# First 2 MB of up weights behind the thirtieth pass: one transfer of 48 rows and ten of 8 rows

## The reference

```python
def moe_ffn(x, w_router, b_router, w_up, b_up, w_down, b_down):
    logits = (x @ w_router + b_router).astype(jnp.float32)
    top_v, top_i = lax.top_k(logits, TOP_K)
    gates = jax.nn.softmax(top_v, axis=-1)
...
    for e in range(N_EXPERTS):
        hid = x @ w_up[e] + b_up[e]
        x_glu = jnp.minimum(hid[..., ::2], SWIGLU_LIMIT)
        x_lin = jnp.clip(hid[..., 1::2], -SWIGLU_LIMIT, SWIGLU_LIMIT)
        act = x_glu * jax.nn.sigmoid(SWIGLU_ALPHA * x_glu) * (x_lin + 1.0)
        out = out + gate_full[:, e:e + 1] * (act @ w_down[e] + b_down[e])
    return out
```

## Time and profile before

| | us |
|---|---|
| median of 3 runs (lowest, highest) | 1095.09 (1094.93, 1096.48) |
| the profiled execution, device time | 1095.05 |
| the profiled execution, span | 1093.3 |
| TensorE matmul busy (share of the span) | 1041.1 (95%) |
| VectorE, ScalarE busy | 254.1, 194.4 |
| SyncE's queue of transfers: bytes, share of 16 engines' span | 427.17 MB, 93.4% |

### The profile page before, as it was taken

One profiled execution on the slowest core, in us unless ns is written; L12 is line 12 of the kernel. 1 busy time (PEld: TensorE's weight loads), 2 busy tenths in 40 slices (PEclk: granted clock), 3 DMA queues, 4 the chain that ended last, 5 costly groups with the idle time before them and its releaser, 6 DMA issues.

```text
span 1093.3 us, 12731 instructions
## 1 busy us (share of the span) xinstructions
PE 1041.1 (95%) x5191; PEld 457.5 (42%) x5191; DVE 254.1 (23%) x660; ACT 194.4 (18%) x365; POOL 8.0 (1%) x25
## 2 busy tenths in 40 slices
PE   8999999999999999999999998999999999999995
PEld 8988564333333333333333333333333333333331
DVE  6887354111111111111111111011111111111113
ACT  5584221111111111111011111011111110111110
POOL 2000000000000000000000000000000000000000
PEclk9999999999999999999999999999999999999998
DMA  9725798999999999999999999999999999999993
GB/s 324 222 77 152 291 403 332 383 430 428 430 427 434 433 429 433 429 432 430 432 430 432 430 432 430 432 430 431 432 427 436 424 437 427 435 430 424 427 423 150
DMA packets 36000, 428.33 MB, mean 392 GB/s; under 512 B 3888, under 2 KB 17232, under 8 KB 20112
## 3 DMA queue, kind: packets, MB, share of 16 engines
q1 hardware_dynamic: 34416, 427.17, 93.4%
q10 hardware_dynamic: 1536, 0.43, 0.2%
HBM read 426.02 MB, written 1.05 MB: 391 GB/s over the span
## 4 chain that ended last, share of the span: by engine, by line
PE 64%; DMA 34%; DVE 1%; ACT 0%; issue 0%; ACTq 0%; DVEq 0%; SPq 0%
DMA ring<-in_w_down_dram 23%; PE bank L1506 22%; PE bank L1570 15%; DMA wbuf<-in_w_down_dram 7%; PE bank L1461 4%; PE bank L1208 4%; PE bank L1446 3%; PE bank L1225 3%; DMA tail_mem<-in_w_down_dram 3%; PE bank L1271 3%; PE bank L1454 1%; PE bank L1550 1%; PE bank L1517 1%; PE bank L1536 1%; PE bank L1189 1%; PE bank L1253 1%
## 5 line engine op out<-in xcount | busy, mean ns | idle before, releaser
L1506 PE MATMUL bank<-ring,wbuf 128*64 128x512 f32 x1248 | 276.9, 594 | 1.9 <-DMA ring<-in_w_up_dram 1.2
L1570 PE MATMUL bank<-ring,wbuf 128*64 128x512 f32 x640 | 146.5, 610 | 18.0 <-DMA ring<-in_w_down_dram 18.0
L1506 PEld LDWEIGHTS bank<-ring,wbuf 128*64 128x64 f32 x1248 | 87.7, 137 | 164.8 <-issue 156.4
L698 ACT ACTIVATE wbuf<-wbuf 128x256 f32<-128x256 f32 x64 | 26.6, 416 | 474.0 <-DVE wbuf L1133 474.0
L1133 DVE TENSOR_SCALAR wbuf<-bank 128x256 f32<-128x256 f32 x64 | 26.8, 420 | 309.3 <-PE bank L1506 309.3
L1117 DVE TENSOR_SCALAR hT<-iota_s,hT 128x128 f32<-128x128 f32 x64 | 19.3, 344 | 334.5 <-PE bank L1536 333.4
L1570 PEld LDWEIGHTS bank<-ring,wbuf 128*64 128x64 f32 x640 | 50.0, 141 | 111.6 <-issue 109.4
L1506 PE MATMUL bank<-tail_mem,wbuf 128*64 128x512 f32 x416 | 93.1, 594 | 0.9 <-DMA tail_mem<-in_w_up_dram 0.9
L1506 PE MATMUL bank<-wbuf 128*64 128x512 f32 x384 | 85.8, 594 | 0.0
L1461 PE MATMUL bank<-wbuf,putT 64*128 64x512 f32 x264 | 65.6, 615 | 1.4 <-ACT wbuf L703 1.4
L1446 PE MATMUL bank<-X,hT 128*64 128x512 f32 x256 | 60.9, 593 | 0.1
(11 more groups left out here) (244 smaller groups left out, 814.6 us busy)
## 6 DMA issues: line engine op xcount, KB each, us to landing
ring<-in_w_up_dram SPq DMA_DIRECT2D x29, 4096.0 KB, 40.8
ring<-in_w_down_dram SPq DMA_DIRECT2D x14, 4096.0 KB, 37.4
ring<-in_w_up_dram SPq DMA_DIRECT2D x20, 2048.0 KB, 16.0
wbuf<-in_w_up_dram SPq DMA_DIRECT2D x10, 4096.0 KB, 40.7
tail_mem<-in_w_up_dram SPq DMA_DIRECT2D x9, 4096.0 KB, 39.6
ring<-in_w_down_dram SPq DMA_DIRECT2D x10, 2048.0 KB, 17.7
wbuf<-in_w_down_dram SPq DMA_DIRECT2D x5, 4096.0 KB, 38.1
tail_mem<-in_w_up_dram SPq DMA_DIRECT2D x8, 2048.0 KB, 19.3
```

The costliest lines, as they stand in the source:

```text
L698: a.activation(sig[:, w], glu[:, w], ACT.Sigmoid, scale=SIG_ALPHA).then_inc(s["sig_ready"], 1)
L1506: ins = mm(bank[n][c * SLOTS:(c + 1) * SLOTS, :], xT[:, k, :], units(row, n, c), start=(k == 0), stop=(k == KT - 1))
L1570: ins = mm(bank[1 if last else 2][c * SLOTS:(c + 1) * SLOTS, :], actT[:, at:at + SLOTS], wk[:, a * D + c * 512:a * D + (c + 1) * 512], sta ...
```

## The change

In the loop, the first of the four up chunks is no longer one transfer of 128 rows but eleven: rows 0 to 47, then ten times 8 rows. All go to the same buffer and raise the same semaphore, each by 16, so TensorE's wait for this chunk asks for 176 a pass where it asked for 16, and the raise before the loop is adapted. The other three up chunks, the down chunks and all passes before are as they were.

```diff
+        ROW_PARTS = [slice(0, 48)] + [slice(r, r + 8) for r in range(48, P, 8)]
...
                 for c in range(UPC):
                     sp.wait_ge(s["chunk_used"], p * CHUNKS + used(up_at(1, c)) - CHUNKS)
-                    sp.dma_start(buffer(UP_HOME[c]), source(e, c)).then_inc(chunk_in[UP_HOME[c]], 16)
+                    for r in ROW_PARTS if c == 0 else [slice(0, P)]:
+                        sp.dma_start(buffer(UP_HOME[c])[r, :], source(e, c)[r, :]).then_inc(chunk_in[UP_HOME[c]], 16)
...
-                pe.wait_ge(chunk_in[UP_HOME[c]], 16 * p + 16)
+                each = 16 * (len(ROW_PARTS) if c == 0 else 1)
+                pe.wait_ge(chunk_in[UP_HOME[c]], each * p + each)
                 return buffer(UP_HOME[c])
...
-            for b in UP_HOME:
-                pe.sem_inc(chunk_in[b], 16 * (FIXED + 1 - seen[b]))
+            for c, b in enumerate(UP_HOME):
+                pe.sem_inc(chunk_in[b], 16 * (len(ROW_PARTS) if c == 0 else 1) * (FIXED + 1) - 16 * seen[b])
```

## The result

The change made the kernel slower: 1111.53 us (median of 4 runs, 1109.02 to 1113.26) against 1095.01 for the kernel before in the same session. The ratio is 1.0156, with a 95% interval of 1.0143 to 1.0169. The forecast was 1092.8 and the range ended at 1098.5. Of these, 1.2 us had been lost before the change begins (its first issue stands at 1023.99, where the one of before stands at 1022.77, a difference between executions); 17.0 us belong to the change.

What follows compares the result with a forecast made beforehand. The prediction took the weight stream's landing at 1062.28, set by the later half of the DMA engines, to bound the end. 5.5 - 3.05 - 0.15 = 2.3 us earlier gave 1095.09 - 2.3 = 1092.8 us; range 1092.3 to 1098.5.

Steps and rivals of the forecast that it cites:

- the price of a row: Weight stream: each 16,384-byte row is one packet done by one engine, 0.611 us a row.
- Where the rows go: Changed chunk: eight engines get 13 rows, the others 3; one half falls back 3.05 us, the other gains 3.05.
- the sum's only term for what the ten transfers cost the engines: Overhead of ten more transfers on the eight engines getting the rows: 0.15 us, bounds 0 and 0.8.
- the eight of an 8-row transfer being all ahead: Main case, chance 0.74: 8-row transfers use the engine half that ends first, so landings come earlier.
- the other half or a mix: Rival, chance 0.20: 8-row transfers include late engines; later landings 3.2 us later, total 1098.3.
- the term of 2.45 us: Landing that stood at 1062.28: 5.5 - 3.05 = 2.45 us earlier, before overhead.
- a shelf of some 11 us at one half: Wrong-half sign at the stream's end: DMA share stays at 0.5 for some 11 us.
- the prediction's instruction fetches: Supposed source of the lag: 31 fetches of 16 KB between 200 and 1070, seemingly all carried by eight engines.
- In a row: Rival, chance 0.01: each 8-row transfer begins when the one before has landed, 2.1 us each; total 1108.
- 0.5 us an issue: SyncE's issues of the split chunk: 0.52 us each, 5.2 us for ten more, hidden by the queue.
- is there well before 1045.11: TensorE's wait on the split first chunk: the chunk lands before TensorE needs it, so no wait.
- The 5.5 us lag: Weight stream: eight of sixteen DMA engines run 5.5 us behind the other eight, and they set each landing.

Runs made afterwards that it cites:

- extra_own: Kernel before plus five additional 8-row transfers into a free buffer, rows four apart within rows 0 to 63; 1097.19 us.
- columns: The change's eleven transfer sizes, but the chunk cut by columns, so each transfer has all 128 rows; 1094.47 us, ratio 0.9996 to the kernel before.
- extra_one: Kernel before plus one additional transfer of 8 neighbouring rows into a free buffer; 1095.42 us, ratio 1.0016.
- pairs_other: Kernel before plus five additional 2-row transfers into a free buffer, rows 64 and 68, 65 and 69 and so on; 1096.02 us, ratio 1.0026.
- pairs_own: Kernel before plus five additional 2-row transfers into a free buffer, rows 0 and 4, 1 and 5 and so on; 1094.61 us, ratio 1.0005.
- spread8: The change, but each of its ten 8-row transfers takes rows ten apart instead of neighbours; 1111.10 us, ratio 1.0158 to the kernel before.
- extra_near: Kernel before plus five additional transfers of 8 neighbouring rows, rows 0 to 39, into a free buffer; 1103.95 us, ratio 1.0088.
- near_far: Kernel before, chunk as rows 64 to 127, then eight 8-row transfers writing neighbouring SBUF rows but reading DRAM rows four apart; 1110.35 us.
- far_near: Kernel before, chunk as rows 64 to 127, then eight 8-row transfers reading neighbouring DRAM rows but writing SBUF rows four apart; 1104.10 us.

## Why the prediction was wrong

**The step that failed** is the price of a row, stated just ahead of "Where the rows go" and used in it: "A row is done by one engine", 4.89 / 8 = 0.611 us a row. I took 0.611 us for a property of the row, whichever engine writes it to whichever partition. The view from which it came has only 128-row transfers, so it can't show this. It should have had an upper bound of its own, as a cost that the trace of before does not show; the sum's only term for what the ten transfers cost the engines was 0.15 us, at most 0.8, and no rival had another. In its place the runs showed packets of 1.20 us in the mean, on all engines, while rows go to other engines' ways. That cost 13.9 us, the change's 17.1 less the 3.2 of extra_own, which has the uneven load alone (13.4 by the model).

The Trainium skill would have given a warning. "SBUF — State Buffer", Door 1, says that the number of ports which a transfer's partitions reach sets its rate, that rows 0 to 63 reach 8 of 16, and that two transfers on two halves are not fused. halves agrees: two transfers of 64 rows cost 12.5 us more than one of 128. Half the rate for this one chunk would be 4.89 us; the rest is that other transfers' packets slow too. On this the Trainium skill, "DMA: Bandwidth & Descriptors", Back-pressure in remote DMA, says that a saturated port clogs the path back to the engines that share it. It says so of transfers between cores. Here loads from DRAM look the same from outside: two crowded engines halved the rate of all sixteen. Whether it is that mechanism no run here shows.

**Which half.** I gave 0.74 to the eight of an 8-row transfer being all ahead and 0.20 to the other half or a mix. It is a mix: six ahead and two behind, by the shelf at 0.12. So the term of 2.45 us that the forecast counted as gained was a loss of 3.06. The mix rival's price of 3.2 us was right (extra_own, 3.2 us); its sign, a shelf of some 11 us at one half, was that of all eight behind and not of a mix. What puts some engines behind, the prediction's instruction fetches or something else, no run tested. That the two classes are exactly half each was no argument against a mix of the eight that a transfer takes.

**In a row**, the rival with 0.01, had a time near the result (1108) by another mechanism. Each small transfer waiting for the one before is excluded by columns, with ten transfers of 128 KB and no loss, and by the full share during the slow stretch. The 2.0 us each that the prediction took from the Trainium skill, "DMA: Bandwidth & Descriptors", and worked out to 23 us, is a fit for single transfers issued by GpSimd; columns shows that it does not add up over transfers in SyncE's queue.

**Fixed cost of ten more transfers.** I took 0.15 us, bounds 0 and 0.8. columns is 0.4 us faster than before with an interval from -1.5 to +0.5. That allows 0 to 0.5 and excludes the upper bound of 0.8; it says nothing finer, and nothing on transfers to fewer engines, for which extra_own's interval (1.9 to 4.5 us, 3.06 of them for the rows) leaves up to 1.4 us for five.

**SyncE.** Right: 0.5 us an issue. That a delay of one transfer's issue is hidden by the queue held too. That the first chunk "is there well before 1045.11" did not: it landed at 1061.2, because of the slow packets and not of SyncE.

**The 5.5 us lag** between two halves of the engines was right, and the runs used it: it stays with an even load (halves), and it makes two dips out of one small transfer (extra_one). The range would have held extra_own, not the change.

No run came out measurably faster than the kernel before. Shifting rows from the late engines to the others means writing on ways that are not theirs, and by the model even one such row costs all engines 0.6 us for the 0.6 it moves.

## What to carry to other kernels

Cut a transfer by columns, not by rows, while others are in flight: 128 rows with a part of each row leave every engine in its place. Watch the issuing engine then: columns' twelve issues took 14.20 us, longer than the stream needs for their bytes, and as far as the trace tells only the lead of half the engines hid it. The price of a badly placed packet is not its own delay but that of all packets beside it, so in a stream that bounds the kernel even a small transfer has to be looked at for where it writes. And read DMA share and GB/s together: few bytes at a low share is starving, few bytes at a full share is slowing.

## What the runs showed of the hardware

- Two engines that write rows 64 and 68, 65 and 69 and so on beside a stream of 128-row transfers take the throughput of all sixteen from 426 to 205-231 GB/s for as long as they do it; rows 0 and 4 and so on take nothing (pairs_other, pairs_own).
- The loss is not deeper with four engines to a way than with two (the change 175 to 266 GB/s, spread8 206 over 8 us and 193 to 258 after it). I had expected it to grow with the number. What in the fabric makes it a factor of two for everybody is not shown by these runs.
- A transfer of 8 rows four apart in rows 0 to 63 beside the stream cost its rows' time only, one engine a row (extra_own).
- SyncE issues transfers of 8 neighbouring rows every 0.5 us (5.64 us for twelve issues in the change), and of 8 rows written four apart every 0.83 us (4.17 us for five in extra_own, against 2.19 in extra_near). It goes by the rows written, not by those read: 5.00 us for ten in near_far, 7.99 in far_near.
- The 14.20 us for twelve issues in columns are no even price: the first six start 0.5 us apart, and two of the later ones took 4.12 and 3.15 us.
